# Weight slabs in six places of two parts, the low part written over the raw data

## The chip, the cores and the metric

One NeuronCore of a Trainium2 chip runs the whole program. The metric is the device time of one execution in microseconds; the inputs and the weights are in HBM at the start.

## What is computed

One inference step of a two-layer encoder for two groups of tokens that share the weights: 1024 tokens of a prompt and 64 tokens of a stream with cached keys and values, 1088 columns in all. Model width is 1024, all in fp32. Each layer is, with an RMS norm ahead of each part and a residual sum behind it:

```python
qa, ka, va, fa, qb, kb, vb = jnp.split(h @ w_in, IN_SPLITS, axis=-1)
o = jnp.concatenate([fox(qa, ka, va, log_sigmoid(fa + b_f)), swa(rope(qb), rope(kb), vb, sinks)], -1)
x = x + o @ w_out[l]                                   # 8 heads with forgetting, 8 heads with a window of 128
x = x + cross_attend(rms_norm(x), w_mq, mk, mv, w_mo)  # 4 heads into 256 memory tokens
gate, val = jnp.split(rms_norm(x) @ w_up, 2, -1)       # width 2816
x = x + (silu(causal_conv3(gate)) * val) @ w_down
```

A last RMS norm gives y; keys, values, log-forget terms, window tails and the conv states are outputs too.

## The kernel before

Everything lies feature-major: a tile holds 128 features on the partitions and the 1088 tokens as columns, worked on in three chunks of 384, 384 and 320. fp32 precision comes from splitting each operand into a high and a low part of type fp32r; TensorE does three products for one (high by high, low by high, high by low). `HH` and `HL` are the parts of the normalised input, `G0H/G0L` and `G1H/G1L` those of the gated feed-forward tiles, `WH` and `WL` those of the weights.

The weights come as half-slabs of 128 x 512 (256 KB), 242 a layer and 484 in all, in the order of their use (`slab_order`, `HALVES`). The cached keys and values travel in the same stream. A slab passes through three engines in four places, slab n in place n % 4:

- SyncE (`load`) brings it into `RAW`. It waits until the split of slab n-4 is done (`w_ready`). The first four loads stand among those of the input, and behind them come the constants and the memory tokens.
- GpSimd (`split`) waits for the load and, from slab 4 on, for the release of slab n-4 (`w_used`). It writes `WH` = RAW + 0 (L586) and `WL` = RAW - WH (L588). It does nothing else in the whole program.
- TensorE waits for `w_ready` (`slab`, `slab_pair`), uses the slab and raises `w_used`.

TensorE's work is in `project` (two slabs in turn, 8 blocks of 128 x 128 against 1088 columns), `project_late` (the second projection behind a norm, with the matmuls of the norm's statistics in its middle), `down` (two slabs for four output tiles) and `attention`, a software pipeline into whose gaps `parts` puts pieces of projections. Matmul results go to two sets of PSUM banks (`free[0]`, `free[1]`) for the first 768 columns and to one shared area for the last 320 (`third_free`), so a tile's last chunk can start only when VectorE has read the one before.

VectorE adds the outputs of `down` to the residual `XT` (L1745; L1576 within the attention), reading PSUM. It makes the low parts: L1614 `HL`, L1548 through the helper `lo`. With the output of a down projection ahead of a norm it also sums squares (L1622, `ACC`), from which the statistics are made: ScalarE writes `QH`, VectorE `QL`, TensorE multiplies both by a matrix of means. In the feed-forward (`gate`, `gated`) it scales the gate tile, does the convolution (L1931 to L1934), multiplies by the norm's factor (L1941 for 1024 columns, L1942 for the 64 of the stream), then by the value tile from PSUM, and makes the low part in two instructions of 1024 and 64 columns. The feed-forward has 22 tiles: two tiles' gate and value projections (`up`), then the down projection of the two tiles before (`mix_down`), FT // 2 - 1 times a layer.

Of the kernel before, what the change touches and what calls it, by code (L numbers as in the profile page):

```python
# [17 lines left out]
F32 = mybir.dt.float32  # L18
F32R = mybir.dt.float32r
# [4 lines left out]
DEPTH, D, SEQ, DEC, PAST = 2, 1024, 1024, 64, 1024  # L24
# [13 lines left out]
HALF = 512  # L38
# [3 lines left out]

FOX_SLABS = 10
N_SLABS = 2 + PAIRS * FOX_SLABS + 8 + (4 + PAIRS * 3) + 8 + 16 + MEM_H * 3 + 8 + FT * 6 + 2
assert N_SLABS % 4 == 0

C_MIX, C_MEM, C_TOK, C_FFN = 0, 8, 16, 24
C_CONV = 32
# [118 lines left out]
HALVES = [(key, place) for key in ORDER for place in PLACES[key]]  # L167
LAYER_SLABS = len(HALVES)
# [3 lines left out]
def encoder_step(nc, xT, memT, slabs, layer_c, final_c, clogf, swa_tail_k, swa_tail_v,  # L172
                 o_y, o_fk, o_fv, o_lf, o_sk, o_sv, o_mk, o_mv, o_cv, o_tk, o_tv):
    ctx = ExitStack()
    with ctx:
        def sem(name):
            return ctx.enter_context(nc.semaphore(name))

        at = [(nc.sbuf_base + 31) // 32 * 32]

        def here(name, shape, dt, offset):
            return nc.alloc_sbuf_tensor_at(name, shape, dt, offset=offset)

        def sb(name, shape, dt=F32):
            size = 4 * int(np.prod(shape[1:]))
            offset = at[0]
            at[0] = offset + (size + 31) // 32 * 32
            return here(name, shape, dt, offset)
# [2 lines left out]
        XT = sb("XT", [128, KT, T])  # L191
        HH0 = at[0]
        HH, HL = (sb(n, [128, KT, T], F32R) for n in ("HH", "HL"))
        RAW = sb("RAW", [128, 4, HALF])
        WH, WL = (sb(n, [128, 4, HALF], F32R) for n in ("WH", "WL"))
        G0H = sb("G0H", [128, 2, T], F32R)
        G0L_AT = at[0]
        G0L = sb("G0L", [128, 2, T], F32R)
# [99 lines left out]

        x_in = [sem(f"x_in{i}") for i in range(KT)]
        ident_in, const_in, mem_in, const_ok, memset_ok = (sem(n) for n in ("ident_in", "const_in", "mem_in", "const_ok", "memset_ok"))  # L300
        raw_in = [sem(f"raw_in{i}") for i in range(4)]
        w_hi, w_ready, w_used = sem("w_hi"), sem("w_ready"), sem("w_used")
        full = [sem("full0"), sem("full1")]
        free = [sem("free0"), sem("free1")]
# [100 lines left out]
        def ended(fill, s, gap):  # L405
            return [part for part, _, last in fill[s][gap] if last] if s in fill else []
# [99 lines left out]
        def step_areas(st):  # L506

            if st["heads"] == 1:
                a, sink = st["pieces"][0][2], st["pieces"][0][6]
                return [(a, a + st["width"] + (sink is not None))]  # L510
            return [(p, p + n + (sink is not None)) for _, _, p, n, _, _, sink in st["pieces"]]
# [24 lines left out]
        def group_areas(tiles):  # L536

            whole = [j for j, (_, rows) in enumerate(tiles) if rows == 128]
            areas = [(128, 0, 128 * len(whole))] if whole else []
            return areas + [(rows, 128 * j, 128) for j, (_, rows) in enumerate(tiles) if rows < 128]  # L540


        @block.sync
        def _(sp):
            sp.dma_start(LCS[:, :, :], layer_c.rearrange("l p n -> p l n")).then_inc(lc_in, 16)
            sp.dma_start(ident_at[:], c_ident).then_inc(ident_in, 16)

            def load(n):
                l, place = divmod(n, LAYER_SLABS)
                sp.dma_start(RAW[:, n % 4, :], slabs[l * N_SLABS + HALVES[place][1]]).then_inc(raw_in[n % 4], 16)  # L550

            load(0)
            load(1)
            for kt in range(KT):
                sp.dma_start(XT[:, kt, :], xT[:, kt, :]).then_inc(x_in[kt], 16)
            load(2)
            load(3)
            for a, b in ((causal, c_causal), (tail_mask, c_tail), (FC, final_c)):
                sp.dma_start(a[:], b).then_inc(const_in, 16)
            sp.dma_start(MR[:, :, :], memT).then_inc(mem_in, 16)  # L560
            for n in range(4, DEPTH * LAYER_SLABS):
                sp.wait_ge(w_ready, n - 3)
                load(n)
            for l in range(DEPTH):
                sp.dma_start(o_tk[l], swa_tail_k[l]).then_inc(out_done, 16)
                sp.dma_start(o_tv[l], swa_tail_v[l]).then_inc(out_done, 16)
            sp.wait_ge(out_done, 16 * (2 * DEPTH + KT))
            sp.wait_ge(lf_out, 16 * DEPTH)
            sp.wait_ge(k32_out, 16 * DEPTH)
            sp.wait_ge(t32_out, 16 + 16 * DEPTH * (2 * PAIRS + 3))  # L570
            sp.wait_ge(co_out, 16 + 16 * DEPTH)


        @block.gpsimd
        def _(pool):
            pool.memset(zero[:], 0.0).then_inc(memset_ok, 1)
            pool.memset(big[:], 3.0e38).then_inc(memset_ok, 1)
            pool.memset(eps[:], EPS).then_inc(memset_ok, 1)
            pool.memset(one[:], 1.0).then_inc(memset_ok, 1)

            def split(n):
                s = n % 4
                pool.wait_ge(raw_in[s], (n // 4 + 1) * 16)
                if n >= 4:
                    pool.wait_ge(w_used, n - 3)
                pool.tensor_tensor(WH[:, s, :], RAW[:, s, :], zero[:, 0:1].to_broadcast([128, HALF]), ALU.add).then_inc(w_hi, 1)  # L586
                pool.wait_ge(w_hi, n + 1)
                pool.tensor_tensor(WL[:, s, :], RAW[:, s, :], WH[:, s, :].bitcast(F32), ALU.subtract).then_inc(w_ready, 1)  # L588

            pool.wait_ge(memset_ok, 4)  # L590
            for n in range(DEPTH * LAYER_SLABS):
                split(n)
# [3 lines left out]
        def _(pe0):  # L596
            place = Place()
# [55 lines left out]
            def slab(pe, key):  # L653

                assert HALVES[place.n["slab"] % LAYER_SLABS][0] == key, (key, HALVES[place.n["slab"] % LAYER_SLABS])
                slot = place.n["slab"] % 4
                pe.wait_ge(w_ready, place.at("slab", 1))
                place.add("slab")
                return slot

            def slab_pair(pe, key):


                assert HALVES[place.n["slab"] % LAYER_SLABS][0] == key, (key, HALVES[place.n["slab"] % LAYER_SLABS])
                slot = place.n["slab"] % 4
                place.add("slab")
                return [slot, slab(pe, key)]

            def project(pe, key, xh, xl, chunks, fresh=None):

                s = claim(pe)
                for half in range(2):
                    slot = slab(pe, key)
                    for ks in ((0, 1), (2,), (3,)):
                        steps = []
                        for k in ks:
                            kt = half * 4 + k
                            if fresh is not None and k == ks[-1]:
                                pe.wait_ge(h_ready, place.at("ntile", fresh + kt + 1))
                            steps.append([(w[:, slot, k * 128:(k + 1) * 128], x[:, kt, :])  # L680
                                          for w, x in ((WH, xh), (WH, xl), (WL, xh))])
                        products(pe, s, steps, chunks, kt == 1, kt == KT - 1)
                    if half == 0:
                        signal(w_used, now=True)
                filled = done(s)
                signal(w_used)
                return filled
# [28 lines left out]
            def down(pe, rows, keys, late=None):  # L716


                slots = None
                for m in range(4 * len(keys)):  # L720
                    s = claim(pe)
                    if m % 4 == 0:
                        slots = slab_pair(pe, keys[m // 4])
                    steps = [[(w[:, slots[r], (m % 4) * 128:(m % 4 + 1) * 128], x)
                              for w, x in ((WH, rows[r][0]), (WH, rows[r][1]), (WL, rows[r][0]))] for r in range(2)]
                    if m == 0 and late is not None:
                        products(pe, s, steps[:1], CH, True, False)
                        pe.wait_ge(*late)
                        products(pe, s, steps[1:], CH, False, True)
                    elif m % 4 < 3:  # L730
                        products(pe, s, steps, CH, True, True)
                    else:
                        products(pe, s, steps[:1], CH, True, False)
                        signal(w_used, now=True)
                        products(pe, s, steps[1:], CH, False, True)
                    done(s)
                    if m % 4 == 3:
                        signal(w_used)
# [1398 lines left out]
```

## Time and profile before

| | |
|---|---|
| three runs | 3405.64, 3419.58, 3424.76 us, median 3419.58 |
| the profiled execution | 3406.41 us, span 3404.6 us |
| busy | TensorE 3238.8, VectorE 1902.6, ScalarE 844.4, GpSimd 1208.5 us |
| TensorE's granted clock | 0.986 of full speed |
| DMA | 177.57 MB, mean 52 GB/s |

The span runs from the first to the last instruction of the profiled execution. Busy time is the sum over an engine's instructions without overlap. An instruction that waits for access while it is already dispatched counts as busy, so a long duration can hold a wait. In a timeline, "x2" means that two instructions in a row are merged in one line; what stands in brackets is the idle time before the instruction and what ended it.

### The profile page before, as it was taken

The numbers are of one execution on the slowest core, as the hardware profiler recorded it, in microseconds if no ns is written. First come the engines' busy times: TensorE is split into PE (matmuls) and PEld (weight loads), VectorE is DVE, ScalarE is ACT, GpSimd is POOL, SyncE is SP. The second block draws the span as 40 slices with busy tenths as digits, with TensorE's granted clock in tenths as the row PEclk, the third lists the DMA queues.
The fourth block names the chain that finished last, engine by engine and source line by source line (L and its number), as shares of the span: only waits on it lengthen the run. The fifth ranks groups of instructions, "written<-read, shape, count | busy, mean of one in ns | idle before, by whom it ended". The sixth has DMA issues, their size and how long they took to land.

```text
span 3404.6 us, 50260 instructions
## 1 busy us (share of the span) xinstructions
PE 3238.8 (95%) x20472; PEld 3119.4 (92%) x20472; DVE 1902.6 (56%) x3552; ACT 844.4 (25%) x1959; POOL 1208.5 (35%) x976
## 2 busy tenths in 40 slices
PE   7999999999999999999999999989899999999997
PEld 6888898888899999999988988988889999999997
DVE  6555567676744444444665655576666444444446
ACT  4432223543310000000233333144433000000002
POOL 4213222632443333334342122334425333334331
PEclk9999999999999999999999999999999999999998
DMA  4111222210111111111122112221111111111111
GB/s 158 48 54 44 57 61 69 66 44 29 37 47 45 44 44 46 42 44 47 41 78 57 45 38 64 75 70 51 47 29 41 45 46 44 44 44 47 44 44 64
DMA packets 86021, 177.57 MB, mean 52 GB/s; under 512 B 10544, under 2 KB 13872, under 8 KB 85392
## 3 DMA queue, kind: packets, MB, share of 16 engines
q1 hardware_dynamic: 71968, 132.90, 13.5%
q10 hardware_dynamic: 13824, 41.46, 4.1%
q8 instruction: 163, 2.67, 0.3%
q14 instruction: 66, 0.54, 0.1%
HBM read 150.36 MB, written 16.29 MB: 49 GB/s over the span
## 4 chain that ended last, share of the span: by engine, by line
PE 80%; DVE 11%; ACT 5%; issue 2%; POOL 1%; DMA 0%; DVEq 0%; SPq 0%; ACTq 0%; POOLq 0%
PE PS L606 80%; DVE ACC L1622 2%; ACT PR L1251 1%; DVE PR L1702 1%; DVE HL L1614 1%; DVE XT L1745 1%; DVE PW L1702 1%; DVE XT L1576 1%; ACT PW L1251 1%; POOL WL L588 1%; ACT PTH L1103 1%; DVE DG L1661 1%; POOL WH L586 0%; DVE PTL L1548 0%; ACT G0H L1103 0%
## 5 line engine op out<-in xcount | busy, mean ns | idle before, releaser
L586 POOL TENSOR_TENSOR WH<-RAW,zero 128x512 fp32r<-128x512 f32 x484 | 549.1, 1134 | 2110.6 <-PE PS L606 2098.3
L606 PE MATMUL PS<-HH,WH 128*128 128x384 f32 (+1 forms) x3312 | 864.8, 333 | 45.7 <-DVE HL L1614 19.2
L606 PE MATMUL PS<-HH,WL 128*128 128x384 f32 (+1 forms) x3312 | 848.2, 328 | 0.0
L606 PE MATMUL PS<-HL,WH 128*128 128x384 f32 (+1 forms) x3312 | 848.0, 328 | 0.0
L588 POOL TENSOR_TENSOR WL<-RAW,WH 128x512 fp32r<-128x512 f32 x484 | 664.4, 1373 | 38.0
L606 PEld LDWEIGHTS PS<-HH,WH 128*128 128x128 f32 x3312 | 587.1, 189 | 66.9 <-issue 23.5
L606 PEld LDWEIGHTS PS<-HL,WH 128*128 128x128 f32 x3312 | 590.0, 188 | 0.0
L606 PEld LDWEIGHTS PS<-HH,WL 128*128 128x128 f32 x3312 | 588.8, 188 | 0.0
L1745 DVE TENSOR_TENSOR XT<-PS,XT 128x320 f32<-128x320 f32 x464 | 314.2, 719 | 265.5 <-PE PS L606 265.5
L606 PE MATMUL PS<-G0H,WH 128*128 128x384 f32 (+1 forms) x960 | 274.6, 339 | 25.5 <-DVE XT L1576 16.9
L1103 ACT ACTIVATE PTH<-PS 128x512 fp32r<-128x512 f32 (+4 forms) x320 | 165.5, 520 | 518.0 <-PE PS L606 516.4
L606 PE MATMUL PS<-G0H,WL 128*128 128x384 f32 (+1 forms) x960 | 264.0, 327 | 0.0
L606 PE MATMUL PS<-G0L,WH 128*128 128x384 f32 (+1 forms) x960 | 263.6, 327 | 0.0
L1921 DVE TENSOR_TENSOR GP<-PS,R 128x256 f32<-128x256 f32 x44 | 18.7, 424 | 377.8 <-PE PS L606 366.6
L1103 ACT ACTIVATE CO<-GP 128x2 f32<-128x2 f32 x88 | 13.1, 195 | 870.9 <-DVE GP L1925 870.9
L1548 DVE TENSOR_TENSOR PTL<-PS,PTH 128x512 fp32r<-128x512 f32 (+4 forms) x320 | 182.5, 587 | 50.9 <-ACT PTH L1103 50.6
L606 PEld LDWEIGHTS PS<-G0H,WH 128*128 128x128 f32 x960 | 170.9, 188 | 41.0 <-DVE XT L1576 24.1
L606 PEld LDWEIGHTS PS<-DG,PR 128*128 128x128 f32 x1296 | 163.1, 201 | 44.9 <-issue 18.5
L606 PE MATMUL PS<-DG,PR 128*128 128x128 f32 x1296 | 180.9, 292 | 20.7 <-DVE PTL L1548 18.4
L606 PEld LDWEIGHTS PS<-G0L,WH 128*128 128x128 f32 x960 | 175.9, 188 | 0.0
L606 PEld LDWEIGHTS PS<-G0H,WL 128*128 128x128 f32 x960 | 174.7, 188 | 0.0
L606 PE MATMUL PS<-PTH,V 128*128 128x128 f32 (+3 forms) x784 | 163.9, 278 | 8.8 <-DVE G0L L1548 5.1
(252 smaller groups left out, 4716.1 us busy)
## 6 DMA issues: line engine op xcount, KB each, us to landing
RAW<-in_slabs SPq DMA_DIRECT2D x484, 256.0 KB, 2.6
XR<-decays ACTq DMA_DIRECT2D x16, 512.0 KB, 5.8
XT<-in_xT SPq DMA_DIRECT2D x8, 544.0 KB, 8.0
out_fk<-T ACTq DMA_DIRECT2D x8, 544.0 KB, 2.7
XR<-decays ACTq DMA_DIRECT2D x16, 272.0 KB, 7.1
out_fv<-T ACTq DMA_DIRECT2D x8, 544.0 KB, 3.1
out_y<-YT ACTq DMA_DIRECT2D x8, 544.0 KB, 3.1
RX<-ST ACTq DMA_DIRECT2D x24, 136.0 KB, 2.6
```

The source lines that it names most:

```text
L586: pool.tensor_tensor(WH[:, s, :], RAW[:, s, :], zero[:, 0:1].to_broadcast([128, HALF]), ALU.add).then_inc(w_hi, 1)
L588: pool.tensor_tensor(WL[:, s, :], RAW[:, s, :], WH[:, s, :].bitcast(F32), ALU.subtract).then_inc(w_ready, 1)
L606: ins = pe.matmul(*a, **k)
L1103: return act.activation(out, in_, ACT.Copy)
L1251: ins = act.activation(p, p, ACT.Exp, bias=NM[:, s % 3, h:h + 1], scale=-1.0, accum_out=SM[:, s % 3, h:h + 1])
L1548: ins = dve.tensor_tensor(out, in_, high.bitcast(F32), ALU.subtract)
L1576: dve.tensor_tensor(XT[:, m, a:b], PS[:, THIRD:THIRD + b - a], XT[:, m, a:b], ALU.add).then_inc(third_free, 1)
L1614: dve.scalar_tensor_tensor(HL[:, m, :], XT[:, m, :], gains[:, m:m + 1], HH[:, m, :].bitcast(F32), ALU.mult, ALU.subtract).then_inc(h_ready, 1)
L1622: dve.tensor_tensor(ACC[:], ACC[:], squares[(m - 1) % SQS], ALU.add).then_inc(sq_used, 1)
L1661: ins = dve.tensor_tensor(DG[:, j % 2, :, :], ident[:].unsqueeze(1).to_broadcast([128, 2, 128]), RC[:, k, :].unsqueeze(2).to_broadcast([12 ...
L1702: ins = dve.tensor_tensor_reduce(probs(st, s % 3, p, p + m), src, bias, -st["scale"], start[:], ALU.add, ALU.min, acc)
L1745: over_tile(place, lambda src, a, b: dve.tensor_tensor(like(XT[:, m, :], a, b), src, like(XT[:, m, :], a, b), ALU.add), last_reader=True)
```

## The change

`RAW`, `WH` and `WL` had four places each. Now `WH` and `WL` have six, and `RAW` is laid over `WL`: the raw data land where the low part will be, and L588 writes the low part over its own input. SyncE can therefore load slab n only when TensorE has released slab n-6, for which it waits (`w_used`); GpSimd waits for the load alone. Loads 4 and 5 have no wait and stand behind the constants.

```diff
-assert N_SLABS % 4 == 0
+SLOTS = 6
...
-        RAW = sb("RAW", [128, 4, HALF])
-        WH, WL = (sb(n, [128, 4, HALF], F32R) for n in ("WH", "WL"))
+        WH = sb("WH", [128, SLOTS, HALF], F32R)
+        WL_AT = at[0]
+        WL = sb("WL", [128, SLOTS, HALF], F32R)
+        RAW = here("RAW", [128, SLOTS, HALF], F32, WL_AT)
...
-        raw_in = [sem(f"raw_in{i}") for i in range(4)]
+        raw_in = [sem(f"raw_in{i}") for i in range(SLOTS)]
...
-                sp.dma_start(RAW[:, n % 4, :], slabs[l * N_SLABS + HALVES[place][1]]).then_inc(raw_in[n % 4], 16)
+                sp.dma_start(RAW[:, n % SLOTS, :], slabs[l * N_SLABS + HALVES[place][1]]).then_inc(raw_in[n % SLOTS], 16)
...
-            for n in range(4, DEPTH * LAYER_SLABS):
-                sp.wait_ge(w_ready, n - 3)
+            load(4)
+            load(5)
+            for n in range(SLOTS, DEPTH * LAYER_SLABS):
+                sp.wait_ge(w_used, n - SLOTS + 1)
                 load(n)
...
             def split(n):
-                s = n % 4
-                pool.wait_ge(raw_in[s], (n // 4 + 1) * 16)
-                if n >= 4:
-                    pool.wait_ge(w_used, n - 3)
+                s = n % SLOTS
+                pool.wait_ge(raw_in[s], (n // SLOTS + 1) * 16)
                 pool.tensor_tensor(WH[:, s, :], RAW[:, s, :], zero[:, 0:1].to_broadcast([128, HALF]), ALU.add).then_inc(w_hi, 1)
                 pool.wait_ge(w_hi, n + 1)
                 pool.tensor_tensor(WL[:, s, :], RAW[:, s, :], WH[:, s, :].bitcast(F32), ALU.subtract).then_inc(w_ready, 1)
...
-                slot = place.n["slab"] % 4
+                slot = place.n["slab"] % SLOTS
```

The last pair of lines stands twice, in `slab` and in `slab_pair`.

## Rows read from the trace of the kernel before

**Rows 1.** Page, busy time and share; windows: us, busy and (x instructions) per engine
```profile
PE 3238.8 (95%) x20472; PEld 3119.4 (92%) x20472; DVE 1902.6 (56%) x3552; ACT 844.4 (25%) x1959; POOL 1208.5 (35%) x976
...
925.00:1680.00 755.00, 755.00 (x4542) 755.00 (x4541) 353.68 (x448) 64.14 (x136) 297.47 (x252) 1.00 0.16 45
```

**Rows 2.** TensorE's waits (total, times, longest); timelines: start, us, instruction, idle before
```profile
PE PS L606 <- POOL WL L588: 10.7, 10, 1.7
...
275.15 1.04 POOL L586 TENSOR_TENSOR WH<-RAW,zero 128x512 fp32r<-128x512 f32 x1 [8.64 <-PE PS L606]
...
287.08 1.04 POOL L586 TENSOR_TENSOR WH<-RAW,zero 128x512 fp32r<-128x512 f32 x1 [7.15 <-PE PS L606]
...
291.88 0.46 PE L606 MATMUL PS<-HH,WH 128*128 128x384 f32 x1 [1.68 <-POOL WL L588]
...
611.50 1.04 POOL L586 TENSOR_TENSOR WH<-RAW,zero 128x512 fp32r<-128x512 f32 x1 [0.20 <-PE PS L606]
...
616.69 1.04 POOL L586 TENSOR_TENSOR WH<-RAW,zero 128x512 fp32r<-128x512 f32 x1 [0.19 <-PE PS L606]
```

**Rows 3.** Splits and loads by source line: ns min/median/max; load to landing, us
```profile
L586 POOL TENSOR_TENSOR WH<-RAW,zero x484: 1032/1040/2192, 5.8 to 3355.1; 128x512 fp32r<-128x512 f32 x162
...
L588 POOL TENSOR_TENSOR WL<-RAW,WH x484: 1260/1294/3158, 6.9 to 3356.3; 128x512 fp32r<-128x512 f32 x162
...
DMA to landing us min/median/max: 2.4/2.6/11.1
```

**Rows 4.** VectorE beside GpSimd: timelines of both at 1622, two source lines
```profile
1622.00 1.27 DVE L1941 TENSOR_TENSOR YY<-YY,R 128x1024 f32<-128x1024 f32 x1 [1.18 <-ACT YY L1474]
1623.19 1.31 DVE L1942 TENSOR_TENSOR YY<-YY,R 128x64 f32<-128x64 f32 x1
...
1622.27 2.15 POOL L588 TENSOR_TENSOR WL<-RAW,WH 128x512 fp32r<-128x512 f32 x1
...
L1942 DVE TENSOR_TENSOR YY<-YY,R x44: 211/213/1315, 941.5 to 3327.7; 128x64 f32<-128x64 f32 x44
...
L1745 DVE TENSOR_TENSOR XT<-PS,XT x464: 476/717/949, 267.6 to 3378.4; 128x320 f32<-128x320 f32 x78, 128x768 f32<-128x768 f32 x77
```

**Rows 5.** Timeline where a value projection ends and a down projection begins (feed-forward)
```profile
1148.18 1.04 POOL L586 TENSOR_TENSOR WH<-RAW,zero 128x512 fp32r<-128x512 f32 x1 [3.76 <-PE PS L606]
...
1149.30 1.31 POOL L588 TENSOR_TENSOR WL<-RAW,WH 128x512 fp32r<-128x512 f32 x1
...
1150.66 1.36 DVE L1548 TENSOR_TENSOR G1L<-YY,G1H 128x1024 fp32r<-128x1024 f32 x2 [1.27 <-ACT G1H L1103]
...
1151.94 0.48 DVE L1745 TENSOR_TENSOR XT<-PS,XT 128x320 f32<-128x320 f32 x1
...
1152.62 0.19 PEld L606 LDWEIGHTS PS<-G0H,WH 128*128 128x128 f32 x1
```

**Rows 6.** Timelines of GpSimd and VectorE in the first norm
```profile
28.00 2.21 POOL L588 TENSOR_TENSOR WL<-RAW,WH 128x512 fp32r<-128x512 f32 x1
35.96 1.36 POOL L586 TENSOR_TENSOR WH<-RAW,zero 128x512 fp32r<-128x512 f32 x1 [5.75 <-PE PS L606]
...
31.28 1.28 DVE L1622 TENSOR_TENSOR ACC<-ACC,SQ 128x1088 f32<-128x1088 f32 x1
...
33.74 2.67 DVE L1622 TENSOR_TENSOR ACC<-ACC,SQ 128x1088 f32<-128x1088 f32 x2
```

**Rows 7.** Timelines of both in the norm ahead of the memory attention
```profile
732.22 2.20 DVE L1614 SCALAR_TENSOR_TENSOR HL<-XT,LCS,HH 128x1088 fp32r<-128x1088 f32 x1
734.34 1.28 DVE L1622 TENSOR_TENSOR ACC<-ACC,SQ 128x1088 f32<-128x1088 f32 x1
...
756.37 2.21 POOL L588 TENSOR_TENSOR WL<-RAW,WH 128x512 fp32r<-128x512 f32 x1
...
758.62 1.29 DVE L1548 TENSOR_TENSOR QL<-ACC,QH 128x1088 fp32r<-128x1088 f32 x1 [1.18 <-ACT QH L1103]
```

**Rows 8.** The diagonal tiles of the attention by source line: ns min/median/max
```profile
L1661 DVE TENSOR_TENSOR DG<-ident_r,RC x128: 424/425/1308, 92.4 to 2548.3; 128x256 f32<-128x256 f32 x128
```

More of the change, by code:

```diff
@@ L664, in slab_pair @@
                 assert HALVES[place.n["slab"] % LAYER_SLABS][0] == key, (key, HALVES[place.n["slab"] % LAYER_SLABS])
-                slot = place.n["slab"] % 4
+                slot = place.n["slab"] % SLOTS
                 place.add("slab")
```

## The prediction

> **What bounds the kernel now.** I read first the busy shares: TensorE is busy 95% of the span, VectorE 56%, GpSimd 35% [rows 1]. The windows say where TensorE is not full: the convolution feed-forward runs it through without a gap (755.00 us of 755.00 in the first layer) [rows 1], so the holes lie in the start, the attention and the normalisations. So this kernel is a stream of matmuls with small holes, and an edit to the weight supply can win the holes that the supply makes and nothing more. The list of waits names them: matmuls waited for the low-part split (L588) 10 times, 10.7 us in all [rows 2]. I checked that this is the whole of it by following one such hole: a matmul starts at 291.88 after 1.68 us of idle time, released by L588, and GpSimd's work on the two slabs for it begins at 287.08, after 7.15 us of waiting for TensorE to give up a place [rows 2]: GpSimd lacks places, not time.
>
> **What the change does, by parts.** Two edits have one answer each. The ring asks for the same memory (12 half-slabs of 2 KB a partition before, 12 after), so no other tile moves. Number and size of loads and splits are the same, 484 loads, 484 high and 484 low parts at 1.04 and 1.29 us [rows 3]; no row shows GpSimd writing over its own input. The nearest are its two forms, which differ by 0.25 us: I take 0 a split, with -0.25 and +0.25 as bounds, on an engine that has 65% of its time free [rows 1]; it would matter only where a split stands against VectorE, below, and there by a tenth of the price.
>
> *The supply.* Before, slab n is split as soon as slab n-4 is released, its raw data being there already. After, SyncE waits for the release of slab n-6, then issues the load. A load takes 2.6 us to landing (2.4 at least, 11.1 at most) [rows 3], and the split 2.4, so a slab is ready 5.1 us after the release of n-6. Behind the new wait on SyncE's queue stand only later slab loads (the constants and the memory tokens go first, the last transfers come at the end), and GpSimd alone waits for those. In the hole of [rows 2] both splits waited for a release (the second ends just before 291.88). The pair before them was split from 275.15 on, the second slab 2.4 us later, so by 277.5 the releases were there on which the new loads wait, and 277.5 + 5.1 = 282.6 is 9 us ahead of the need at 291.88. The tightest supply is that of the memory tiles: two slabs are released every 5.2 us (splits at 611.50 and 616.69, [rows 2]). There a pair needs 2.6 + 0.1 + two splits of 2.4 = 7.5 us and has twice 5.2, so 2.9 to spare. I followed all ten holes so, and none is left: 10.7 us go. What is late next there is nothing of the supply. Term: -10.7, bounds -10.7 and -8 (another wait close behind).
>
> *When the splits run.* This is the part that the short description leaves out. The splits move: from 0.13 us behind a release to 2.7 us behind one (2.6 of load, some 0.1 of hand-over). VectorE and GpSimd hold each other up. In [rows 4] VectorE's product of two SBUF tiles starts at 1622.00, GpSimd's low part at 1622.27 takes 2.15 us in place of 1.29, and then VectorE's 64-wide product at 1623.19 takes 1.31 us, where its median is 0.21 (L1942). They take turns by whole instructions; a waiting GpSimd goes next. Reads from PSUM aren't touched: the 464 residual adds (L1745) never take over 0.95 us, splits beside them or not [rows 4]. The Trainium skill, SBUF — State Buffer, "Who interferes with whom", states the same as a rule (an exclusive lock on a shared port pair, issue order decides, DVE instructions with two SBUF inputs take part) and says that the loser blocks for the whole instruction; by that a high part would cost the full 1.04 us where I take 0.85 from the row, which would make the feed-forward term 18 us and not 14. So what matters is which VectorE operations stand where the splits now come.
>
> *Feed-forward, before each down projection.* Look at [rows 5]. The last value tile releases its slab at about 1148.05; GpSimd splits from 1148.18 to 1150.61. VectorE's low part of the gated tile (L1548, two SBUF inputs, 1024 and then 64 wide) starts at 1150.66, 0.05 us after GpSimd is done. Behind it stands the residual add of the first down tile; its 320-wide piece starts at 1151.94 and ends at about 1152.42, and TensorE's next weight load for that same PSUM area is at 1152.62. So TensorE has 0.20 us here, some 0.06 of it hand-over: 0.14 of slack. After the change the split comes at 1148.05 + 2.7 = 1150.8, 0.1 us after the 1024-wide instruction has started. It waits for that, then holds VectorE's 64-wide one back. The row for that costs 1.10 us with a low part; a high part is 0.25 shorter, so 0.85. Less slack: 0.71 us of TensorE stall. There are 10 such places a layer (one group of four projections and a down projection each, FT/2 - 1 groups), 20 in all: +14.2. Bounds: 0, if the small instruction slips ahead of the waiting split; 20 x 1.75 = +35, if the load lands 0.15 us sooner, so that the high part is first, blocks the wide instruction, and the low part the narrow one. The load's own spread (2.4 to beyond 2.6) reaches over that point. I take the middle since the typical load lands behind VectorE's start.
>
> *Start.* Slabs 4 and 5 are no longer held for a release. Before, split 4 ends at 30.2 and 5 comes at 35.96 [rows 6]. After, 5 follows 4 at 30.25, and 6 follows 5 (slab 0 is released at 22). From 31.28 to 36.4 VectorE has a high/low part and three sums that run free (1.28 for the first sum, 2.67 for the last two) where GpSimd's own turns took 2.21 while they alternated [rows 6] and a contended part takes 2.20 [rows 7]. Four GpSimd instructions among them: 0.8 + 1.0 + 0.8 + 0.9 = +3.5. The chain of statistics hangs on these sums, and TensorE waits for it. The split before QL (contended already) is replaced by slab 7's: no difference. Term +3.4, bounds 0 and +5.
>
> *Normalisations with a down projection ahead* (mem and feed-forward in each layer, mix in the second: 5). In [rows 7] a contended high/low part takes 2.20 at 732.22, the sum behind it 1.28 free at 734.34. With splits 2.6 us later the free one meets the second low part, +1.1. At the end, the low part of 756.37 (2.21 us) ends just before QL at 758.62, which takes 1.29; 2.7 us later its low part meets QL, +0.9. In exchange the sums in the middle lose at most one contact. I take +1.5 each: +7.5, bounds 0 and +10.
>
> *Attention.* DG (L1661) takes 0.43 us free and 1.31 held up [rows 8], and there the new times fall as they will: +3 for the longer overlap, bounds -3 and +8, nearer to zero since most of its 128 stand outside any split.
>
> **Sum.** -10.7 + 14.2 + 3.4 + 7.5 + 3 = +17.4 us. Against the profiled execution's own 3406.4 us that is 3423.8. The median of the three runs is 3419.58 (3405.64 to 3424.76); the profiled one stands 13 below it, within that scatter, so I put the difference on the median: 3437.0.
>
> **Rivals.**
> *A: the split slips.* The small instruction at 1151.8 goes ahead, or the stall is eaten by slack: no feed-forward term. Against it: [rows 4] shows the waiting split served first. Then +3.2: 3423.
> *B: only the holes.* Contention moved about but summing to nothing: -10.7, 3409. For it: in the normalisations the splits overlap as many sums as before, and VectorE idles 44% of the time. This is the other side, faster, though below what can be told apart. To reach beyond 0.5% the change would have to win more than all waits for splits, so contention would have to fall.
> *C: the split comes first.* The load lands before 1150.66, blocking both instructions: feed-forward +35, total +38: 3458. It decides from a release-to-split time of 2.6 us or less; the expected one is 2.7.
> *D: the prefetch doesn't do what it says.* A load of 11.1 us (the largest in [rows 3], at the start where inputs flow in) or releases in bunches make the wait on SyncE the late thing. The tightest place has 2.9 us to spare, so it needs loads over 5.5 us in mid-run, where the traffic is a third of the start's. It would cost a few us each: 3450 and more.
>
> **How the numbers follow.** Forecast 0.45, A 0.24, B 0.15, C 0.11, D 0.05. A measurement of this kernel can tell about 0.5% from no change, 17 us. The forecast lies on that line, so it gives 0.26 to slower and 0.19 to same; A is same; B gives 0.10 to same and 0.05 to faster; C and D are slower. Sum: faster 0.05, same 0.53, slower 0.42. The range reaches from B (3407) to C (3459); D and the far tail of B stay out.
>
> **What would show it.** Right: no matmul waits for L588; TensorE's feed-forward windows no longer full, with ten gaps of 0.7 us a layer in front of the last chunk of the second down tile, waiting for L1745; the 64-wide L1548 behind the gated tile at some 1.1 us and not 0.2; L1941 shorter than its 2.34. Wrong: feed-forward windows still gapless (A or B), gaps of 1.7 (C), or waits of GpSimd for the load that matmuls wait for in turn (D). The start: TensorE's statistics matmul at 43 us, not 39.9.

## The result, and the profile after

The changed kernel takes 3437.57 us (median of 7 runs, 3433.47 to 3440.91), the kernel before 3410.72 (7 runs, 3405.09 to 3424.76): a ratio of 1.0083, with a 95% interval of 1.0071 to 1.0095. It is slower by 27 us. The profiled execution has a span of 3436.2 us.

First the waits of the changed kernel (total, times, longest), which answer to [rows 2]. Lines of this kernel stand two higher than before: L588 and L590 are the high and the low part of the split, L1550 was L1548, L1616 was L1614, L1747 was L1745.

```profile
POOL WH L588 <- DMA RAW<-in_slabs: 2024.9, 345, 45.2
...
PE PS L608 <- DVE QL L1550: 25.2, 9, 6.5
PE PS L608 <- DVE XT L1747: 24.6, 32, 1.5
PE PS L608 <- DVE XT L1578: 23.9, 44, 1.8
PE PS L608 <- DVE HL L1616: 22.2, 3, 15.1
```

No line has a matmul waiting for a split any more; the 10.7 us of [rows 2] are gone, and GpSimd waits for its loads instead of for releases. What the matmuls wait for now is VectorE. The same view of the kernel before has, for QL and the residual adds:

```profile
PE PS L606 <- DVE QL L1548: 17.7, 8, 6.5
...
PE PS L606 <- DVE XT L1745: 9.3, 7, 1.5
```

QL costs 25.2 us where it cost 17.7, the residual adds 24.6 over 32 waits where it was 9.3 over 7. The change filled the holes of the supply and opened others behind VectorE.

The windows (us, then busy time and instructions of PE, PEld, DVE, ACT and POOL; TensorE's granted clock as a share; DMA) show where: the start, the feed-forward of the first layer and the norm at the seam of the layers.

```profile
0.00:45.00 45.00, 21.59 (x102) 20.75 (x103) 31.36 (x21) 20.54 (x19) 28.64 (x24) 0.92 0.48 178
...
940.00:1690.00 750.00, 745.37 (x4469) 742.19 (x4468) 342.99 (x440) 60.43 (x129) 344.11 (x248) 1.00 0.15 44
...
1724.00:1800.00 76.00, 68.86 (x368) 64.96 (x367) 42.66 (x57) 23.05 (x33) 35.21 (x22) 0.84 0.26 75
```

The feed-forward was gapless [rows 1]; now 4.6 us of matmul time are missing from 750 (the releases, below, fall back by 7.1 us in that layer). GpSimd is busy 344 us there, with splits that took 297 before [rows 1]: it is itself held up.

This is the place of [rows 5] in the changed kernel, VectorE, GpSimd and TensorE:

```profile
1160.53 2.21 DVE L1550 TENSOR_TENSOR G1L<-YY,G1H 128x1024 fp32r<-128x1024 f32 x2 [1.27 <-ACT G1H L1105]
1160.61 2.05 POOL L588 TENSOR_TENSOR WH<-RAW,zero 128x512 fp32r<-128x512 f32 x1 [3.83 <-DMA RAW<-in_slabs]
...
1162.66 1.34 DVE L1747 TENSOR_TENSOR XT<-PS,XT 128x320 f32<-128x320 f32 x2
...
1163.19 0.41 PE L608 MATMUL PS<-G0H,WH 128*128 128x320 f32 x1 [0.37 <-DVE XT L1747]
...
1163.19 0.19 PEld L608 LDWEIGHTS PS<-G0H,WH 128*128 128x128 f32 x1 [0.69 <-DVE XT L1747]
```

The split starts 0.08 us behind VectorE's low part. It waits for the 1024-wide instruction (its 1.04 us become 2.05), then has its turn ahead of the 64-wide one: the pair takes 2.21 us where it took 1.36. The residual add comes 0.85 us later against its predecessor, and the weight load that needs its PSUM area waits 0.69 us.

One of the twenty places came out as rival C has it. At 1595 the load landed in 2.48 us, the high part started 0.05 us ahead of VectorE, and both of VectorE's instructions were held up: the pair took 3.28 us and the weight load waited 1.76. In 18 of the 20 places VectorE's instruction starts 2.61 us behind the release that lets the load go, and the split 2.56 to 2.78.

```profile
1595.18 1.04 POOL L588 TENSOR_TENSOR WH<-RAW,zero 128x512 fp32r<-128x512 f32 x1 [2.66 <-DMA RAW<-in_slabs]
...
1595.23 3.28 DVE L1550 TENSOR_TENSOR G1L<-YY,G1H 128x1024 fp32r<-128x1024 f32 x2 [1.27 <-ACT G1H L1105]
...
1598.96 0.19 PEld L608 LDWEIGHTS PS<-G0H,WH 128*128 128x128 f32 x1 [1.76 <-DVE XT L1747]
```

To see where the time goes I took the moment at which TensorE releases the same slab in both traces; the table gives by how much a kernel is later (+) or earlier (-) than the kernel before. Slab 10 is the end of the first projections, 44 that of the first layer's FoX attention, 83 lies near the end of the windowed one; the feed-forward starts at 118, and its last such gap is at 234. Slabs 252, 286 and 360 are 10, 44 and 118 of the second layer; 483 is the last slab of all.

```
slab        before at    changed  gate_ffn  gate_start  gate_norm  gate_all  gate_chosen  lo_later  four_late
10             94.1       +8.3      +5.6       0.0        +4.8       +1.1       +3.0       +6.0       +1.2
44            422.5       +0.2      -2.3      -6.8        -2.9       +1.6       -4.9       -1.4      +11.2
83            685.6       +0.1      -2.7      -7.1        -3.0       +4.2       -5.3       -1.7      +23.1
118           962.3       +8.7      +6.1      +2.8        -1.3       +4.3       -4.1       +6.8      +38.0
234          1661.2      +15.8      +6.1     +12.2        +7.1       +4.3       -4.2       +6.8      +44.3
252          1773.6      +24.5     +11.9     +17.0        +8.1       +4.3       -3.7      +15.7      +49.1
286          2102.0      +17.1      +7.8      +9.3        +0.4       +4.2      -11.5      +10.1      +56.7
360          2641.6      +25.3     +15.4     +17.1        +4.5       +4.3       -8.3      +19.3      +83.7
483          3385.2      +31.6     +15.4     +24.6       +12.0       +4.4       -8.3      +19.2      +92.3
```

Each column is one profiled execution, so a microsecond or two of it is scatter (the last input landed between 17.0 and 18.8 us). The shape of the first column isn't: up at the start, down in each FoX attention, up in the norms, and up in the feed-forward. There it rises at every twelfth slab, 0.59 to 0.65 us each time, but for 0.82 at slab 392 and 1.70 at slab 222, the place at 1595.

### The profile page after: what moved, and what is told of

Read it like the earlier page. It is cut to its first block, busy times and chain, and to the rows that moved or that the text cites. A ratio compares the mean times of both kernels' runs of the same rounds, so it can differ in the third digit from the quotient of the medians.

```text
span 3436.2 us, 49780 instructions
## 1 busy us (share of the span) xinstructions
PE 3249.0 (95%) x20472; PEld 3123.5 (91%) x20472; DVE 1921.8 (56%) x3552; ACT 845.5 (25%) x1959; POOL 1316.3 (38%) x976
## 3 DMA queue, kind: packets, MB, share of 16 engines
q8 instruction: 163, 2.67, 0.3%
## 4 chain that ended last, share of the span: by engine, by line
PE 76%; DVE 15%; ACT 6%; issue 2%; DMA 0%; DVEq 0%; SPq 0%; ACTq 0%
PE PS L608 76%; DVE ACC L1624 2%; ACT PR L1253 1%; DVE PR L1704 1%; DVE HL L1616 1%; DVE XT L1747 1%; DVE PW L1704 1%; DVE G0L L1550 1%; ACT G0H L1105 1%; DVE XT L1578 1%; DVE DG L1663 1%; ACT PW L1253 1%; DVE G1L L1550 1%; DVE YY L1948 1%; DVE QL L1550 1%
## 5 line engine op out<-in xcount | busy, mean ns | idle before, releaser
L588 POOL TENSOR_TENSOR WH<-RAW,zero 128x512 fp32r<-128x512 f32 x484 | 606.4, 1253 | 2025.0 <-DMA RAW<-in_slabs 2024.9
L590 POOL TENSOR_TENSOR WL<-RAW,WH 128x512 fp32r<-128x512 f32 x484 | 715.3, 1478 | 37.9
L1747 DVE TENSOR_TENSOR XT<-PS,XT 128x320 f32<-128x320 f32 x464 | 313.9, 718 | 260.7 <-PE PS L608 260.6
L1550 DVE TENSOR_TENSOR PTL<-PS,PTH 128x512 fp32r<-128x512 f32 (+4 forms) x320 | 182.2, 586 | 48.5 <-ACT PTH L1105 48.4
```

Of the source, the lines that this page charges most:

```text
L1550: ins = dve.tensor_tensor(out, in_, high.bitcast(F32), ALU.subtract)
L1747: over_tile(place, lambda src, a, b: dve.tensor_tensor(like(XT[:, m, :], a, b), src, like(XT[:, m, :], a, b), ALU.add), last_reader=True)
```

## The experiments

The theory on record was one of timing: the splits do the same work, but 2.7 us behind a release in place of 0.13, and what they meet there on VectorE costs more than the holes gave. The main rival was that the new layout costs by itself: the low part written over its input, loads that come late, more places.

### The old moment in the new layout

Each of the first four puts the wait of before back into the changed kernel's split; they differ in its condition.

```diff
                 pool.wait_ge(raw_in[s], (n // SLOTS + 1) * 16)
+                if n >= 4 and (CONDITION):
+                    pool.wait_ge(w_used, n - 3)
```

CONDITION is `True` for gate_all, `n % 242 >= 118` for gate_ffn, `n < 12` for gate_start, and for gate_norm

```
n % 242 in range(90, 98) or n % 242 in range(110, 118) or 242 <= n < 250
```

> Six places and the low part over the raw data as in the changed kernel, but each split from slab 4 on also waits for the release of slab n-4, as before the change. Theory of timing (the loss comes from when GpSimd's splits run against VectorE): the splits start 0.13 us behind a release again, VectorE's instructions are held up where they were, and the ten waits for a split come back: within 3 us of the kernel before (3410.7), and the feed-forward windows full (755 of 755 us). Rival (the loss lies in the memory layout, in the write over its own input, or in loads that come late): stays near 3437.6.

Measured: 3409.55 us, ratio to the kernel before 0.9996 (0.9983 to 1.0009). In the trace the matmuls wait for the split again, 10 times, exactly as in [rows 2], and the feed-forward has no gap (its line of the waits, and its window):

```profile
PE PS L610 <- POOL WL L592: 10.7, 10, 1.7
```

```profile
935.00:1680.00 745.00, 745.00 (x4483) 745.00 (x4482) 348.77 (x442) 60.42 (x129) 295.21 (x251) 1.00 0.16 45
```

This kernel has the six places, the low part written over the raw data, and loads that wait for TensorE. It differs from the changed kernel only in when a split may start, and 28 us are gone. (The old wait also gives up the two places of lead; lag5_all below keeps one of them.) So the rival falls: the layout costs nothing that can be measured here, the moment costs all of it.

> The changed kernel, with the wait for slab n-4's release put back for the feed-forward's slabs alone (place 118 and later of each layer). Theory of timing: the 20 gaps of 0.6 us ahead of the second down tile go, so some 12 to 14 us less than the changed kernel: 3424. Rival (gaps in the feed-forward come from something else, or the gain is given back in the next norm): 3437.

Measured: 3421.47 us, 1.0029 (1.0016 to 1.0042): 16.1 less than the changed kernel, 12 to 14 expected. In the table the lag stands still from slab 118 to 234 (6.1 and 6.1) and from 360 to 483. The feed-forward's gaps are a term of their own and pass on to the end in full. They are not all of the 16.1: the table has 7.1 and 6.3 us in the two feed-forwards of the changed kernel, and of the rest 2.9 at the seam (slab 234 to 252), where both kernels split late and the changed one ran 6.8 us longer at the lower clock.

> The changed kernel, with the old wait put back for slabs 4 to 11 alone. The changed kernel is 7.6 us late at the release of slab 6, of which some 1.2 us is the load of the inputs. If the start's loss passes on to the end: 3437.6 - 6 = 3431. Rival: the first layer's attention, which shows the lag shrink from 8.3 us to 0.2 us, takes it up anyway, and nothing is won: 3437.

Measured: 3429.38 us, 1.0057 (1.0042 to 1.0072): 8.2 less. The start's loss passes on in full too. The attention gives the changed kernel 8 us, but gives gate_start nearly as much (0.0 to -6.8): it isn't the start's loss that is made up there.

> The changed kernel, with the old wait put back around the five norms that follow a down projection (places 90 to 97 and 110 to 117 of each layer, and the first eight slabs of the second layer). By the lags of the two traces the norms cost 5.0, 2.4, 5.3, 3.2 and 2.6 us, 18.5 in all. Theory of timing, each passing on to the end: 3437.6 - 18.5 = 3419. Rival (my term of the prediction, 7.5 us; the rest is lost elsewhere or given back by the attention behind): 3430.

Measured: 3416.22 us, 1.0018 (1.0008 to 1.0027): 21.4 less, which is nearer to the 18.5 of the lags than to my own term of 7.5. This is the largest of the three, and the one that I had priced worst. Two things make it up. The first is in the rows that answer to [rows 7]:

```profile
744.62 4.38 DVE L1616 SCALAR_TENSOR_TENSOR HL<-XT,LCS,HH 128x1088 fp32r<-128x1088 f32 x2
748.92 10.16 DVE L1624 TENSOR_TENSOR ACC<-ACC,SQ 128x1088 f32<-128x1088 f32 x5
760.26 2.21 DVE L1550 TENSOR_TENSOR QL<-ACC,QH 128x1088 fp32r<-128x1088 f32 x1 [1.18 <-ACT QH L1105]
```

QL takes 2.21 us, where it took 1.29: the +0.9 of the prediction, to the digit, and the two high/low parts take 4.38 in place of 4.02. The second I had left out. Here are the ten microseconds behind it, first of the kernel before, then of the changed one, with a second window of that further on:

```profile
759.00:769.00 10.00, 8.83 (x53) 8.51 (x54) 3.56 (x4) 5.72 (x6) 1.23 (x1) 1.00 0.11 26
```

```profile
760.00:770.00 10.00, 7.48 (x35) 7.48 (x36) 3.56 (x3) 5.81 (x7) 1.26 (x1) 0.83 0.00 0
790.00:800.00 10.00, 7.76 (x52) 7.36 (x51) 8.40 (x25) 5.54 (x18) 6.59 (x6) 0.83 0.19 54
```

TensorE's granted clock is 0.83 of full speed in both windows of the changed kernel, that is a third of them at the lower level of 1.2 GHz, and full before. It fell behind a wait of 3.1 us for QL, which was 1.8 us in the kernel before. Over each whole trace, without the last stretch at its end, TensorE runs at the lower level for:

```
             start  FoX 0  norms 0  norm at seam  FoX 1  rest   sum (us)
before        13.7   17.1    3.4       10.2        17.1   10.2   71.7
changed       20.5    6.8   10.2       23.9        10.2   13.7   85.3
gate_norm     13.7    6.8    3.4        6.8         6.8   17.1   54.6
gate_chosen   17.1    6.8    3.4        6.8         6.8   17.1   58.0
four_late     10.2   20.5   17.1       13.7        13.7   58.0  133.1
clear_both    17.1    6.8    0.0        6.8         6.8    6.8   44.4
```

A microsecond at half speed costs half of one where TensorE is the bound. By that the norms of the changed kernel lose some 3.4 us in the first layer and 6.9 at the seam to the clock, and both FoX attentions together win 8.6.

In the norms the loss of clock goes with the late splits in all twelve traces. The five kernels whose splits are late in the norms (changed, gate_ffn, gate_start, lo_later, four_late) spend 10.2 to 17.1 us at the lower level in the first layer's norms and 13.7 to 23.9 at the seam; the seven others spend 0 to 3.4 and 6.8 to 10.2.

### Adding up, and one place less

gate_chosen has the old wait in all three places at once (`n < 12`, the norms and the feed-forward). lag5_all has it for every slab, one place later:

```diff
+                if n >= 5 and (True):
+                    pool.wait_ge(w_used, n - 4)
```

> The changed kernel with the old wait in all three places at once (start, norms, feed-forward), so that only the attention and the projections near it keep the earlier splits. If the three savings add up (16.1 + 8.2 + 21.4 us of 3437.6): 3392. If the six places win no more than the waits for splits that the trace of before shows (10.7 us against gate_all's 3409.6): 3399. Rival (the attention gave the losses back, so the savings overlap): 3405 or more.

Measured: 3399.24 us, 0.9968 (0.9953 to 0.9982). The three savings make 45.7 us one by one and 38.3 together. Of the two explicit numbers the 3399 was right: against gate_all, which has the holes, it wins 10.3 us, the size of the waits for splits. That this agrees with 10.7 is partly luck, since more than holes goes into it: by the table the two FoX attentions win 15.7 us (+3.0 to -4.9 and -3.7 to -11.5), and the rest takes a part back.

> The changed kernel, but each split from slab 5 on waits for the release of slab n-5. The load for it was let go by the release of n-6 and has landed, so splits start 0.13 us behind a release, as before the change, and still one place earlier. Theory of timing: the moment against VectorE counts and not the lead, so feed-forward and norms are as before the change, and the holes are filled by one place more: 3409.6 - 10.7 + 2 (slab 5 is split at once behind slab 4 at the start) = 3401. Rival (lead itself costs, by splits that come in other numbers into the norms): 3415 or more.

Measured: 3402.36 us, 0.998 (0.9967 to 0.9993), no matmul waiting for a split, no gap in the feed-forward:

```profile
930.00:1670.00 740.00, 740.00 (x4451) 739.91 (x4450) 345.78 (x439) 60.55 (x129) 291.17 (x248) 1.00 0.16 45
```

It splits every slab one release earlier than the kernel before and has no cost for it. So one place of lead is harmless, and it is the distance to the release that decides. The likely reason is that VectorE's work is tied to the same moments: both follow the end of a tile on TensorE.

### The late moment without the extra places

```diff
-SLOTS = 6
+SLOTS = 4
...
-            load(4)
-            load(5)
```

> Four places of two parts, the low part over the raw data: the changed kernel's late load, without its extra places. A split runs 2.7 us behind the release of slab n-4. Theory of timing: the feed-forward has the same 20 gaps of 0.6 us (it asks which moment, not which slab), the norms lose much the same, and each of the ten holes grows by 2.7 us: 3437.6 + 10.7 + 27 = 3475, a little less for the start, where slab 5 is held as before. Rival (six places themselves cause the feed-forward gaps): its feed-forward windows are full.

Measured: 3500.98 us, 1.0265 (1.0247 to 1.0283), 26 more than expected. What it was made for came out as expected: in the feed-forward it loses 6.3 us in ten steps from slab 118 to 234, as the changed kernel does with another slab at the same moment, except at slab 222. In the second layer two of its ten places lose 1.7 us. The window of ten groups but the first, and its waits:

```profile
1010.00:1690.00 680.00, 676.74 (x4058) 673.88 (x4057) 302.84 (x394) 52.80 (x115) 315.35 (x226) 1.00 0.16 44
```

```profile
PE PS L606 <- POOL WL L588: 45.7, 14, 4.3
PE PS L606 <- DVE XT L1745: 26.0, 32, 1.5
```

The waits for splits grew from 10.7 to 45.7 us, 35 where I had expected 27. For the remaining 18 the clock is the likely cause: 133 us at the lower level against the changed kernel's 85, which costs 24 by the half. I had not counted it here either, and no run holds the clock fixed.

### The instruction that is in the way

In lo_later the changed kernel's VectorE does its first residual add before the low part of the second gated tile, not behind it (the helper returns the low part, and the down projection calls it after its first tile).

```diff
-                        gates(dve, turn * 4 + 2 * (b + 1), 1 - b)
-                        down(dve)
+                        down(dve, between={0: gates(dve, turn * 4 + 2 * (b + 1), 1 - b)})
```

> The changed kernel, with VectorE's low part of the second gated tile of each group moved behind the first residual add of the down projection. TensorE needs it 19 us later at the earliest. The held-up instruction no longer stands ahead of the area that TensorE waits for, so if it is the cause the 20 gaps of 0.6 us go: 3437.6 - 13 = 3425. Rival: the gap only moves to the third down tile, whose residual add now stands behind it: 3437, with the wait seen one tile later.

Measured: 3420.55 us, 1.0023 (1.0011 to 1.0035): 17.0 less than the changed kernel, 13 expected (12.4 between the two traces, of which lo_later's is the slowest of its eight executions). The same two low-part instructions are still held up, and nobody waits (timeline of VectorE, then the window):

```profile
1157.65 1.36 DVE L1747 TENSOR_TENSOR XT<-PS,XT 128x320 f32<-128x320 f32 x2 [1.49 <-PE PS L608]
1158.92 2.23 DVE L1550 TENSOR_TENSOR G1L<-YY,G1H 128x1024 fp32r<-128x1024 f32 x2
1161.07 1.35 DVE L1747 TENSOR_TENSOR XT<-PS,XT 128x320 f32<-128x320 f32 x2
```

```profile
940.00:1690.00 750.00, 750.00 (x4512) 750.00 (x4511) 344.03 (x445) 63.96 (x133) 342.04 (x252) 1.00 0.16 45
```

The pair takes 2.23 us as in the changed kernel (2.21), GpSimd is as busy (342 us), and TensorE has no gap. This separates contact from cost: VectorE and GpSimd may hold each other up as much as they like where VectorE has slack.

### Splits kept out of the norms

If the moment decides, there should be a better one than that of before. clear_norm is gate_chosen, but around each of the five norms the first four slabs are split as early as they can be, and the next four wait until the second slab of the norm's first projection is released. clear_both holds slab 4 at the start too.

```diff
+                if base is not None:
+                    if place - base >= 4:
+                        pool.wait_ge(w_used, n - (place - base) + 2)
+                elif n in (4, 5):
+                    pool.wait_ge(w_used, 2)
+                elif 5 < n < 12 or place >= 118:
+                    pool.wait_ge(w_used, n - 3)
```

`base` is 90 or 110 for slabs of these eight of a layer, 0 for slabs 242 to 249; clear_norm has `n - 3` in place of `2`.

> As gate_chosen (old wait for slabs 4 to 11 and in the feed-forward), but around the five norms the splits are moved out of VectorE's chain: the first four slabs of each are split as early as the six places allow, the next four wait until the second slab of the norm's first projection is released. Theory of timing: the 14 us between that projection's first release and its last, where VectorE's low parts and sums are held up five times by 0.6 to 1.1 us in the kernel before, run free, at 1.3 us more in the down projection ahead: 2.5 to 3 us a norm, 3399.2 - 13 = 3386. Rival (the chain waits for ScalarE or TensorE as soon as VectorE is quicker): 3397.

> clear_norm, with slab 4 at the start held until slab 1 is released, together with slab 5. Four of VectorE's instructions in the first norm's chain then run without one turn of GpSimd each way less: two turns of 0.8 and 1.0 us: 1.8 us less than clear_norm. Rival (the chain is then bound by the landing of the inputs and ScalarE's squares): no difference.

Measured: clear_norm 3390.72 us, 0.9953 (0.9936 to 0.9969); clear_both 3389.29 us, 0.9944 (0.9929 to 0.9958). Both beat the kernel before and the changed one, clear_both by 0.56 and 1.4%. In the norm ahead of the memory attention the five sums take 6.87 us, where they took 10.16 with splits among them, and TensorE has no gap beside them (14.00 of 14). Timelines of VectorE and GpSimd, then the window:

```profile
740.82 6.87 DVE L1633 TENSOR_TENSOR ACC<-ACC,SQ 128x1088 f32<-128x1088 f32 x5
748.87 1.29 DVE L1559 TENSOR_TENSOR QL<-ACC,QH 128x1088 fp32r<-128x1088 f32 x1 [1.18 <-ACT QH L1114]
...
749.16 1.90 POOL L597 TENSOR_TENSOR WH<-RAW,zero 128x512 fp32r<-128x512 f32 x1 [19.81 <-PE PS L617]
```

```profile
738.00:752.00 14.00, 14.00 (x86) 14.00 (x84) 10.55 (x9) 4.61 (x4) 2.76 (x2) 1.00 0.18 57
```

The gain over gate_chosen is 8.5 us of the expected 13; the chain got shorter, and then the matmuls of the projection beside it are the bound. The two differ by 1.4 us, which these runs don't tell from nothing, so whether slab 4's hold is worth something stays open.

## Why the prediction was right or wrong

The time on record, 3437.0, agrees with the 3437.57 measured, but by less merit than it looks. The sum said +17.4 us against the kernel before, and the difference is +26.9; it was put on a median of three runs, 3419.58, which seven runs put at 3410.72. The two errors cancel. The difference lies past the bound of 0.5%, on the side that I had given 0.42, while I had given 0.53 to no change. By its terms:

- *The supply, -10.7.* Right: no matmul waits for a split, and gate_chosen against gate_all wins 10.3 us. Rival D played no part; [rows 3] gave the load right, GpSimd started when it should.
- *The feed-forward, +14.2.* Right in mechanism, place and size. The pair of low parts is 0.85 us longer as worked out from [rows 4]; the stall is 0.59 to 0.65 us in 18 of the 20 places, where I had 0.71, 1.70 in one and 0.82 in one. The twenty steps make 13.4. Undoing them won 16.1, of which some 3 lie at the seam. That the high part is served ahead of the 64-wide instruction was the choice between the forecast and A, and the row decided it rightly. Between the forecast and C no row decides, but the landing of each load: the split came 0.08 us behind VectorE at 1160 and 0.05 ahead of it at 1595. The 2.6 us at which the prediction saw C begin is the 2.61 of the traces. By the rule of the Trainium skill (SBUF — State Buffer, "Who interferes with whom") the term would have been 18: the traces agree with it in who takes part and that whole instructions block, but the loss to a part of 1.04 us was 0.85. (The Trainium skill says "fully blocks" of VectorE's 2-port modes there; the exclusive lock it states for all.)
- *The start, +3.4.* Mis-sized: 7.6 us of lag at slab 6, and 8.2 won by undoing it. The rows that answer to [rows 6] hold the counted part:

```profile
32.44 2.13 DVE L1624 TENSOR_TENSOR ACC<-ACC,SQ 128x1088 f32<-128x1088 f32 x1
34.49 2.35 DVE L1616 SCALAR_TENSOR_TENSOR HL<-XT,LCS,HH 128x1088 fp32r<-128x1088 f32 x1
36.77 4.43 DVE L1624 TENSOR_TENSOR ACC<-ACC,SQ 128x1088 f32<-128x1088 f32 x2
```

  The sums at 33.74 that took 2.67 for two take 4.43, a sum and a high/low part 2.13 and 2.35 against 1.28 and 1.34 before: 3.6 us, the term as predicted. The statistics matmul comes at 44.0 us (43 forecast), with inputs that landed 1.2 us later and a QL of 1.61 us where it was 2.23. What the sum missed stands further on. The splits of slabs 8 to 10 now meet VectorE's running sums of the forget gates and the instruction behind them (timelines of the kernel before, then of the changed one, VectorE, GpSimd and TensorE):

```profile
60.23 1.25 DVE L1818 TENSOR_SCALAR C<-C 8x2112 f32<-8x2112 f32 x1
```

```profile
65.26 2.30 DVE L1820 TENSOR_SCALAR C<-C 8x2112 f32<-8x2112 f32 x1
...
65.16 1.29 POOL L590 TENSOR_TENSOR WL<-RAW,WH 128x512 fp32r<-128x512 f32 x1
...
69.34 0.41 PE L608 MATMUL PS<-HH,WH 128*128 128x320 f32 x1 [1.83 <-DVE QLS L1559]
```

  The `TENSOR_SCALAR` waits for the low part that began 0.10 us ahead of it. TensorE waits 1.83 us for what comes behind on VectorE and did not wait before. The same wait (1.7 to 1.9 us) stands in gate_ffn, gate_norm, lo_later and four_late, whose splits are late there too, and in none of the seven other traces. The last 1.7 us to slab 6 go by the half with a stretch of 3.4 us at the lower clock from 70.2 on. gate_ffn, gate_norm and lo_later, which start just as the changed kernel does, lack that stretch and are 3.9 to 6.0 us late at slab 6, not 7.6.
- *The norms, +7.5.* The step that failed most: 21.4 us. The contacts were found: in the first of the five the down projection ahead comes out 1.3 us later (1.1 forecast) and QL takes 0.9 more; TensorE's wait for it grows by 1.3. But a longer wait of TensorE was priced at its own length alone. Behind these waits the clock fell, at 763 and 794, and at the seam for 13.7 us more than before; by the half that is 10.3 us against the kernel before, and 12 of the 21.4 against gate_norm.
- *The attention, +3.* Wrong in sign: -8.1 and -7.4 us in the two FoX attentions, of which the filled holes are 4.2. I had looked for VectorE's DG [rows 8], whose waits are the same before and after (11.4 us). What changed is the clock: 17.1 us at the lower level become 6.8, and 17.1 become 10.2. These two windows of the kernel before and one of the changed kernel show it:

```profile
182.00:200.00 18.00, 15.98 (x85) 13.57 (x84) 8.09 (x19) 6.18 (x18) 4.27 (x5) 0.72 0.16 58
410.00:424.00 14.00, 12.32 (x71) 10.80 (x72) 6.64 (x15) 4.03 (x13) 1.92 (x3) 0.76 0.14 49
```

```profile
410.00:424.00 14.00, 11.75 (x90) 10.39 (x90) 7.93 (x22) 4.63 (x14) 4.62 (x4) 1.00 0.19 61
```

  90 matmuls in 14 us at full clock, 71 at 0.76. That the filled holes are what keeps the clock up there is argued, not shown. The twelve traces speak for it in the first layer: the three kernels with holes (before, gate_all, four_late) have 17.1 to 20.5 us at the lower level in its FoX attention, the nine without 6.8 to 13.7. In the second layer the two groups overlap (13.7 to 17.1 against 6.8 to 17.1), and no run changed the clock alone.

So two things were missing from the sum. One stands in two terms of opposite sign: what a hole in TensorE's work does to its granted clock. The trace of before showed such stretches (a clock of 0.72 and 0.76 in the windows above) and I had not asked what stood ahead of them. The other is a meeting of the two engines behind the first norm that I had not looked for.

Rival A (the split slips) is refuted by the rows at 1160. Rival C (the split comes first) is refuted as the rule but not as an event: it happened in one of the twenty places here, in four of gate_start's, three of gate_norm's and two of four_late's, for some 1.1 us more each time. In all ten the split started 0.01 to 0.07 us ahead of VectorE. Rival B is refuted as a forecast of the change, but names what it would have been with the old moment: gate_chosen, 3399, where B said 3409 on the median of three, or 3400 on that of seven.

## What to carry to other kernels

A deeper buffer also moves the work that refills it. Before adding places, look at what each engine does in the microseconds behind the new moment, above all where two engines hold each other up and one of them is a few tenths of a microsecond from being waited for; a place ahead can be had without the new moment by one more wait (lag5_all), and the moment can be chosen (clear_norm). Where two instructions start within 0.1 us of each other, take both orders as possible and weight them, since a load's landing decides place by place. And price a new wait of TensorE with the clock that follows it, or say that the sum leaves it out.

## What the runs showed of the hardware

- GpSimd and VectorE take turns by whole instructions, both ways, where VectorE's instruction has two SBUF inputs: a high part goes from 1.04 to 2.05 us, a pair of low parts from 1.36 to 2.21. A `TENSOR_SCALAR` of 8x2112 with one tensor in SBUF takes part too (1.25 to 2.30 us, L1820). The shift also took contacts away. This is the source line of the feed-forward's product (ns min/median/max) before and after; its median fell from 2.34 to 1.22 us, and no matmul came sooner for it.

```profile
L1941 DVE TENSOR_TENSOR YY<-YY,R x44: 1215/2342/2345, 939.5 to 3325.4; 128x1024 f32<-128x1024 f32 x44
```

```profile
L1943 DVE TENSOR_TENSOR YY<-YY,R x44: 1210/1225/2308, 949.2 to 3356.2; 128x1024 f32<-128x1024 f32 x44
```

- Writing the low part over its own input costs GpSimd nothing: 1.262 us at least and 1.292 in the median, against 1.260 and 1.294 in [rows 3].
- TensorE's granted clock was at its lower level for 44 to 133 us of some 3400 in these kernels. It scatters between executions of much the same work: gate_all has 85.3 us of it against 71.7 before, with a profiled execution 4.4 us later, at a median that is the same.
